# Delta rule: masked levels in two buffers, masked one level ahead

## The reference, cut to what matters

```python
def gated_delta_rule(q, k, v, g, beta):
    ...
    decay = jnp.exp(jnp.where(causal, gc[..., :, None] - gc[..., None, :], -jnp.inf))
    k_beta = k * beta[..., None]
    lmat = jnp.where(strict, jnp.einsum('bnhcd,bnhed->bnhce', k_beta, k) * decay, 0.0)
    t_inv = lax.linalg.triangular_solve(eye + lmat, jnp.broadcast_to(eye, lmat.shape),
                                        left_side=True, lower=True, unit_diagonal=True)
    u = jnp.einsum('bnhce,bnhed->bnhcd', t_inv, v_beta)
    w = jnp.einsum('bnhce,bnhed->bnhcd', t_inv, k_beta * jnp.exp(gc)[..., None])
    ...
```

## The kernel before, in words

| pair | order on GpSimd |
|---|---|
| 0 | mask 0, low 4, masks 1, 2, 3, low 1, 2, mask 4, low 3, mask 5, low 4, mask 6 |
| 1 | low 1, 2, mask 0, low 3, 4, masks 1, 2, 3, 4, low 1, 2, mask 5, low 3, mask 6, low 4 |
| 2 | mask 0, low 1, 2, mask 1, low 3, mask 2, low 4, masks 3, 4, 5, low 1, 2, mask 6, low 3, 4 |
| 3 | mask 0, mask 1, low 1, 2, mask 2, low 3, mask 3, low 4, masks 4, 5, 6, low 1 to 4 |

## Time and profile before

### The profile page before, as it was taken

How to read it: one execution, slowest core, us unless ns; L and a number is a source line. 1 busy time by engine, 2 the same in 40 slices (tenths; PEclk the granted TensorE clock), 3 DMA queues, 4 the chain that set the end, 5 groups by cost and what they waited for, 6 DMA issues and landing times. The chain is left out here.

```text
span 3153.6 us, 38382 instructions
## 1 busy us (share of the span) xinstructions
PE 2899.1 (92%) x15496; PEld 2345.0 (74%) x15496; DVE 1298.7 (41%) x1946; ACT 996.9 (32%) x1488; POOL 994.3 (32%) x478
## 2 busy tenths in 40 slices
PE   6889886789999998899998989999899999999998
PEld 3767775668888887879545768888677877886686
DVE  7856555551182134530234236411354454203523
ACT  3245543233211212412114323222333333325432
POOL 1221221112232222654002424444243444342342
PEclk9989897789999999999998999999999999999999
DMA  6400100311152123432431225332211011121121
GB/s 238 144 27 14 47 28 1 133 68 54 68 184 76 54 94 112 147 109 91 137 97 67 83 111 193 134 107 86 89 54 41 29 39 41 54 100 46 55 87 67
DMA packets 48531, 268.60 MB, mean 85 GB/s; under 512 B 5633, under 2 KB 6913, under 8 KB 27649
## 3 DMA queue, kind: packets, MB, share of 16 engines
q1 hardware_dynamic: 48384, 266.55, 24.3%
HBM read 264.43 MB, written 2.10 MB: 85 GB/s over the span
## 5 line engine op out<-in xcount | busy, mean ns | idle before, releaser
L420 POOL TENSOR_TENSOR shared_w_lo<-stage,shared_w_hi 128x2048 fp32r<-128x2048 f32 (+1 forms) x127 | 555.9, 4378 | 1246.9 <-ACT shared_w_hi L391 1246.9
L582 POOL TENSOR_TENSOR shared_w_lo<-stage,shared_w_hi 128x512 fp32r<-128x512 f32 (+2 forms) x233 | 297.2, 1305 | 612.5 <-ACT shared_w_hi L574 612.5
L391 ACT CAST shared_w_hi<-stage 128x2048 fp32r<-128x2048 f32 (+1 forms) x127 | 224.3, 1767 | 282.1 <-PE f_acc L484 183.2
L906 DVE TENSOR_TENSOR ffn_hidden<-f_acc,ffn_gate 128x512 f32<-128x512 f32 x66 | 37.7, 599 | 397.2 <-PE f_acc L484 389.1
L484 PE MATMUL f_acc<-norm_b_hi,shared_w_hi 128*128 128x512 f32 (+1 forms) x672 | 174.0, 340 | 0.0
L484 PE MATMUL f_acc<-norm_b_lo,shared_w_hi 128*128 128x512 f32 (+1 forms) x672 | 173.5, 339 | 0.0
L484 PE MATMUL f_acc<-ffn_hi,shared_w_hi 128*128 128x512 f32 (+1 forms) x528 | 159.7, 356 | 1.0 <-DVE ffn_lo L910 1.0
L484 PE MATMUL f_acc<-ffn_lo,shared_w_hi 128*128 128x512 f32 (+1 forms) x528 | 159.4, 356 | 0.0
L649 PE MATMUL two_acc<-norm_f_hi,shared_w_hi 128*128 128x512 f32 (+1 forms) x312 | 129.5, 415 | 9.0 <-DVE norm_f_lo L778 9.0
L896 ACT CAST ffn_hi<-ffn_hidden 128x768 f32 (+3 forms) x44 | 32.0, 728 | 332.9 <-DVE ffn_hidden L906 332.9
L574 ACT CAST shared_w_hi<-stage 128x1024 fp32r<-128x1024 f32 (+2 forms) x117 | 114.7, 1023 | 53.0 <-PE last_acc L649 42.9
(11 more groups left out here) (594 smaller groups left out, 6692.1 us busy)
## 6 DMA issues: line engine op xcount, KB each, us to landing
stage<-in_w_f0i SPq DMA_DIRECT2D x22, 1024.0 KB, 4.9
stage<-in_w_f1i SPq DMA_DIRECT2D x22, 1024.0 KB, 4.9
stage<-in_w_rv SPq DMA_DIRECT2D x16, 1024.0 KB, 4.9
mod_slots_a<-in_w_mod SPq DMA_DIRECT2D x24, 512.0 KB, 6.3
stage<-in_w_rqk SPq DMA_DIRECT2D x12, 1024.0 KB, 5.0
mod_slots_f<-in_w_mod SPq DMA_DIRECT2D x24, 512.0 KB, 3.6
mod_slots_e<-in_w_mod SPq DMA_DIRECT2D x24, 512.0 KB, 5.5
stage<-in_w_dqkv SPq DMA_DIRECT2D x12, 1024.0 KB, 4.9
```

What stands on the lines that cost most here:

```text
L391: nc.scalar.copy(w_hi[:, slot, 0:size], stage[:, slot, 0:size]).then_inc(hi_ready, 1)
L420: nc.gpsimd.tensor_tensor(w_lo[:, slot, 0:size], stage[:, slot, 0:size], w_hi[:, slot, 0:size].bitcast(F32), ALU.subtract)\
L582: last = nc.gpsimd.tensor_tensor(w_lo[:, index % 2, part], stage[:, index % 2, part], w_hi[:, index % 2, part].bitcast(F32), ALU.subtract)
L906: last = nc.vector.tensor_tensor(hidden[:, s:s + m], res[1][:, b, 0:m], gate[:, s:s + m], ALU.mult)
```

## The change

`k_unit[a]` is free once the unit keys have been multiplied, so it becomes a second buffer for the masked levels. Even levels go to `join[a]` and odd ones to `k_unit[a]`. Level m then waits for the half step of level m-2 rather than m-1, level 2 instead of level 1 waits for VectorE's reading of level 0, and level 1 waits only for `lower`. Mask m moves in GpSimd's program to the place of half step m-2, and masks 0 and 1 both stand at `kq`. The number of instructions, their shapes and their results stay.

```diff
+        def level_of(a, m):
+
+            return (join, k_unit)[m % 2][a][:]
...
                     for m in range(7):
-                        more.upto(place(p, f"half{m - 1}" if m else "kq"))
+                        more.upto(place(p, f"half{m - 2}" if m >= 2 else "kq"))
                         for a in range(2):
                             pool.wait_ge(d["lower"], 2 * p + a + 1)
-                            if m:
-                                pool.wait_ge(d["half"], 14 * p + 2 * (m - 1) + a + 1)
-                            if m == 1:
+                            if m >= 2:
+                                pool.wait_ge(d["half"], 14 * p + 2 * (m - 2) + a + 1)
+                            if m == 2:
                                 pool.wait_ge(d["next"], 14 * p + a + 1)
-                            nc.gpsimd.tensor_tensor(chunks(join[a][:]), chunks(low[a][:]), over_chunks(levels[:, m, :]),
+                            nc.gpsimd.tensor_tensor(chunks(level_of(a, m)), chunks(low[a][:]), over_chunks(levels[:, m, :]),
                                                     ALU.mult).then_inc(d["join"], 1)
...
-                        mm = nc.tensor.matmul(ch(banks[a][0], c), ch(join[a], c), ch(inv_t[a], c), start=True, stop=True)
+                        mm = nc.tensor.matmul(ch(banks[a][0], c), ch(level_of(a, m), c), ch(inv_t[a], c), start=True, stop=True)
```

## The result

| | before | changed |
|---|---|---|
| runs, us | 3155.13, 3155.21, 3162.05, 3162.72 | 3120.71, 3130.34, 3132.78, 3139.27 |
| median, us | 3158.63 | 3131.56 |
| span of the profiled execution, us | 3153.6 | 3128.3 |
| its granted clock | 0.958 | 0.959 |

The ratio of the changed kernel to the kernel before is 0.9901, with a 95% interval of 0.9877 to 0.9924: faster by 1.0%, 31 us (24 to 39). The forecast was 25.6 us. By the spans of the two profiles it is 25.3 us. The median of the changed kernel lies in the range of the prediction, 3128 to 3148 us, but the ratio applied to the median before gives 3127.4 us, 0.6 us under its low end. So the sign and the main mechanism came out as forecast, and the size is what the rest of this text is about.

The account below looks back on a forecast made before the run. TensorE, busy 92% of the span, was taken to bound the kernel. Gains of 13.36 + 14.16 = 27.5 us, less 0.7 (late update) and 1.2 (side by side), gave 25.6 us: 3136.5 us, range 3128 to 3148.

Parts of the forecast that it names:

- What bounds the kernel, and where: Delta rule stage: TensorE sets the time; its largest wait is for masks queued behind low pieces, 20.3 us in nine waits.
- The slow clock behind a wait: Levels 4, 5, 6 in pairs 0, 1, 2: each wait goes with its slow clock, 14.16 us in sum.
- Rival 1: The slow clock stays and only the waits are returned: 6.9 us less gain, 3143.4 us; chance 0.10.
- Level 1: All four pairs: mask 1 follows mask 0 at once, so wait and lengthening fall away, 13.36 us in sum.
- the term: Pair 0, side by side: a level 0 subtraction now lies beside a low piece, loss 0 to 0.5 us, 0.2 taken.
- rival 2: Level 1 stays bound by VectorE's update; only levels 4 to 6 pay, 14.16 us: 3147.9 us; chance 0.07.
- VectorE idle ahead of that step: 0: Pair 3, side by side: VectorE is idle ahead of the level 1 step, so mask 1 costs 0 there.
- my upper end: Pair 0, side by side: at most 0.5 us lost by a level 0 subtraction beside GpSimd.
- What is moved past what: Mask 1 ahead of low pieces delays them by 2.5 to 3.4 us, costed at nothing; no new wait is added.
- Rival 4: Slower: TensorE waits for late low parts of its cover, 46 us against 27.5 gained: 3180.5 us; chance 0.05.
- the range's low end: 3128 us: the full 27.5 us taken from the lowest run, 3155.2 us.
- the 8.4 us: Whole kernel: span 3153.6 us stands 8.4 us under the median of the runs, 3162.05; difference carried over unchanged.

Follow-up runs that it names:

- levels 2 to 6 alone: Changed kernel with only masks 2 to 6 made ahead, mask 1 at its old place with the old waits, against the kernel before: ratio 0.9963, 11.7 us.

## Why the prediction was right or wrong

**What bounds the kernel, and where.** Right. TensorE sets the stage's length, the masks held it up, and at levels 4 to 6 and in pairs 1 and 2 at level 1 the cause was the place in GpSimd's program behind low pieces. The run with both buffers at the old places shows that it is the place.

**The slow clock behind a wait.** Right, to 0.2 us, for the trace that the forecast was made from: the half steps of levels 4 to 6 take 2.58 us at 1.00, and each of them gave back its wait and 1.9 us more (1.7 forecast). Rival 1 is out as a forecast, but what I held against it, "each fall follows a wait of 2.8 us or more", was misread: the fall at 2429.2 us in the same trace follows none. Nor does each such wait bring a fall, as the later traces show.

**Level 1.** Pairs 1, 2 and 3 gave 2.4, 5.4 and 1.7 us (2.6, 5.5 and 1.7). In pair 2, VectorE's two products of SBUF arrays beside mask 1 took 0.99 and 0.94 us instead of 0.69, 0.55 us in all where I had taken 0.7:

```profile
2540.13 0.99 DVE L2787 TENSOR_TENSOR y_a<-y_a,dn_gate 128x512 f32<-128x512 f32 x1
...
2541.88 0.94 DVE L2787 TENSOR_TENSOR y_a<-y_a,dn_gate 128x512 f32<-128x512 f32 x1
```

In pair 0 the term was mis-sized: I bounded the loss by 0.5 us and took 0.2, and both subtractions of the mask were slowed, by 0.64 and 0.47 us, so that TensorE waited 1.0 us for VectorE and 0.5 of the 1.7 us were gained. (In the other four traces the first is slowed less, 0.81 us long, and 1.1 us are gained.) The first of them lies beside mask 1 and low piece 4, the second beside that piece and mask 2: GpSimd is now busy all through VectorE's chain, and I had reckoned with the piece only. This is rival 2 in one pair of four.

In pair 3 the term was put at nothing, "VectorE idle ahead of that step: 0", and the trace shows otherwise. Mask 1 (2641.33 to 2644.28 us) lies there beside VectorE's two products, which take 1.36 and 0.92 us instead of 0.69:

```profile
2641.79 1.36 DVE L2787 TENSOR_TENSOR y_a<-y_a,dn_gate 128x512 f32<-128x512 f32 x1
...
2643.91 0.92 DVE L2787 TENSOR_TENSOR y_a<-y_a,dn_gate 128x512 f32<-128x512 f32 x1
```

The update of level 0 is still in time, but ScalarE waits for the first product before it overwrites the gate (2643.24 us, L2613) and with that empties an accumulator, and TensorE waits 0.6 us for it. All five traces of the changed kernel have this wait, and none of the kernel before, nor the one with levels 2 to 6 alone, where mask 1 comes later.

The rule of the Trainium skill that I weighed (Advanced Engine Details and Errata, GPSIMD Details, the interface shared with VectorE) holds in pair 0 at more than my upper end.

**What is moved past what.** Right. No wait for a low part is new, and mask 2 of pair 2 wasn't waited for. Rival 4 is out.

**The size.** Wrong here. The step that failed is the one from the trace to the time, and in it the range's low end: I took 27.5 us, the masked steps of one trace, as the most that the change can give, set it off against the lowest of three runs, and so costed slow clock away from the waits at nothing. The runs show this in its place.

- I took one profiled execution for the kernel, and it was of the cheap form: 493.8 us of stage, where half of the traces have 500 to 503. A profile is one draw. In the trace with 503.2 us the matmuls of the two window rows cost 3.3 + 3.1 us more than in the first trace. Against the cheap form the changed kernel's slow stretches took 4.7 of the 24.8 us away. Against the dear form, which has them too, the stage gains 25.3 to 29.0 us, more than my 27.5 in the dearest trace.
- I carried the 8.4 us between span and median over as a constant. The profiled run of the changed kernel has a span of 3128.3 and a time of 3130.34 us, 2.0 apart; so the rest of the 8.4 was the distance of a short execution from the median.

The measured 31 us lie in an interval (24 to 39) that holds the forecast 25.6, and the estimate missed the range by 0.6 us. That the forecast lies so near to the 25.9 us by which the mean spans of all traces differ is in part luck: its sum knew neither of the two forms nor of the wait in pair 3.

**What stays open.** The times give 31 and 33.5 us (24 to 39 and 28 to 39), and 27 with the two products ahead of the stage; the traces give 23.1 us in the stage and 1.0 behind it on the mean. Ahead of the stage the code is the same and the traces differ by 1.7 us on the mean, with a spread of 20. The traces' 24 to 26 us lie in the first interval and under the second. Some of the difference may be how often the dear form comes in executions that left no trace; six and five traces don't settle it.

## What to carry to other kernels

If an engine's program is written out by hand, ask of each producer what stands in front of it and what that waits for: here 1.25 us masks cost 20 us, since they stood behind weight pieces that waited for a third engine. A second buffer left at the old places paid nothing that could be measured; the earlier place did, and whether it would pay without the buffer is open. Ask also what an engine made busy earlier now runs beside, in every pair and not only where the answer seems close. Charge a wait of TensorE of 2.8 us or more with the slow clock behind it (1.7 to 1.9 us per half step here, in 21 of 24 cases), and take such a sum to a time only over several traces, since one may be in the cheaper of two forms.

## What the runs showed of the hardware

- The granted clock fell in the same stretches of the changed kernel in all five traces, from pair 1 to the end of the stage, and two products of 1.9 us ahead of the stage didn't move them. Some of the stretches stand without any wait in front: in pairs 2 and 3 they begin at matmuls that use 8 rows of the array (L2973, 8*128 by 512 columns), and so does one in the kernel before (2429.2 us). Whether these matmuls are the reason, and why the stretches of pairs 2 and 3 are at 1.00 in three of six traces of the kernel before and in none of the five of the changed kernel wasn't tested.
- GpSimd's mask and VectorE's product of two SBUF arrays slow each other. The product or subtraction goes from 0.69 us to between 0.81 and 1.65; two masks go from 2.52 to 2.98 or 3.41 us. VectorE's subtractions with one input in PSUM (L2847) in the same stretches stayed at 0.67 to 0.69 us.
- Starts of the same stage in executions of the same code ahead of it lay between 2208 and 2229 us in eleven traces.
